# Smaller first loads, idle transposes ahead of the first product, and transposes and one projection placed earlier in a two-layer hybrid attention block

## The reference

```python
h = rms_norm(x, g_mix)                    # 256 x 1024
parts = split(h @ w_in)                   # w_in: 1024 x 10656
# branch A: sliding window attention, 8 heads, 2 key heads, rotary, per-head sinks
# branch B: low-rank q (384) and kv (256), up-projected by b_w_uq and b_w_ukv, 8 heads
# branch C: three dilated groups of 8 heads, combined by their softmax denominators
# branch M: 4 heads over rms_norm(mem) @ m_w_kv, mem of 256 x 1024, the same in both layers
y = stack([o_a, o_b, o_c, o_m]) @ w_branch                    # 4 x (512 x 1024)
x = x + (sum over branches of sigmoid(gate_pre + b_gate) * y) @ w_out
u = rms_norm(x, g_mlp) @ w_up                                 # 1024 x 4096
x = x + square(relu(u)) @ w_down                              # 4096 x 1024
```

## Time and profile before

| | us |
|---|---|
| median of 3 runs (1258.76 to 1259.2) | 1259.02 |
| profiled execution | 1258.06 |
| its span, first to last instruction | 1256.3 |
| PE busy in the span | 1231.5 (98%) |
| PE weight load busy | 1018.6 (81%) |
| DVE busy | 784.9 (62%) |
| ACT busy | 702.1 (56%) |
| POOL busy | 150.0 (12%) |
| DMA moved | 202.6 MB, mean 161 GB/s |

### The profile page before, as it was taken

How to read it: one execution, slowest core, us unless ns; L and a number is a source line. 1 busy time by engine, 2 the same in 40 slices (tenths; PEclk the granted TensorE clock), 3 DMA queues, 4 the chain that set the end, 5 groups by cost and what they waited for, 6 DMA issues and landing times.

```text
span 1256.3 us, 17554 instructions
## 1 busy us (share of the span) xinstructions
PE 1231.5 (98%) x6256; PEld 1018.6 (81%) x6256; DVE 784.9 (62%) x1222; ACT 702.1 (56%) x1086; POOL 150.0 (12%) x127
## 2 busy tenths in 40 slices
PE   7999999999999999999999999999999999999997
PEld 5788888887788878888788888888877887888886
DVE  6756768876556754444567656888655666444543
ACT  6666766654454455555566677665545454555542
POOL 6301333300000000000021113332000000000000
PEclk9999999999999999999999999999999999999999
DMA  8554545454447546656554544445544455556652
GB/s 230 188 151 123 167 129 157 151 167 145 128 130 219 178 147 185 194 184 185 177 152 154 170 140 148 121 154 168 163 141 124 147 177 182 153 185 188 191 184 71
DMA packets 110932, 202.60 MB, mean 161 GB/s; under 512 B 9984, under 2 KB 18176, under 8 KB 110848
## 3 DMA queue, kind: packets, MB, share of 16 engines
q1 hardware_dynamic: 106880, 194.12, 50.6%
q10 hardware_dynamic: 3424, 7.34, 1.7%
q0 software_dynamic: 544, 0.03, 0.1%
HBM read 200.41 MB, written 1.05 MB: 160 GB/s over the span
## 4 chain that ended last, share of the span: by engine, by line
PE 95%; DVE 2%; ACT 1%; DMA 0%; issue 0%; POOL 0%; SPq 0%; ACTq 0%; DVEq 0%
PE ps_d L1333 23%; PE ps_d L1335 22%; PE ps_d L1334 22%; PE ps_b L1333 5%; PE ps_b L1334 5%; PE ps_b L1335 5%; PE ps_b L1413 5%; PE ps_b L1367 4%; PE ps_b L1386 4%; PE ps_b L1392 2%; DMA early<-in_inv_freq_dram 0%; ACT w_hi L916 0%; DVE w_lo L1078 0%; POOL root L870 0%; ACT h_hi L992 0%
## 5 line engine op out<-in xcount | busy, mean ns | idle before, releaser
L1078 DVE TENSOR_TENSOR w_lo<-raw,w_hi 128x1024 fp32r<-128x1024 f32 (+3 forms) x380 | 450.9, 1191 | 327.1 <-ACT w_hi L916 326.1
L916 ACT ACTIVATE w_hi<-raw 128x1024 fp32r<-128x1024 f32 (+3 forms) x380 | 390.9, 1029 | 457.1 <-PE ps_d L1335 345.6
L1333 PE MATMUL ps_d<-w_hi,h_hi 128*128 128x512 f32 (+3 forms) x704 | 287.3, 408 | 3.7 <-DVE w_lo L1078 3.7
L1335 PE MATMUL ps_d<-w_hi,h_lo 128*128 128x512 f32 (+3 forms) x704 | 268.7, 382 | 0.0
L1334 PE MATMUL ps_d<-w_lo,h_hi 128*128 128x512 f32 (+3 forms) x704 | 267.6, 380 | 0.0
L1333 PE MATMUL ps_d<-w_hi,r_hi 128*128 128x512 f32 (+1 forms) x552 | 220.3, 399 | 3.7 <-DVE r_lo L1216 3.5
L1335 PE MATMUL ps_d<-w_hi,r_lo 128*128 128x512 f32 (+1 forms) x552 | 214.6, 389 | 0.0
L1334 PE MATMUL ps_d<-w_lo,r_hi 128*128 128x512 f32 (+1 forms) x552 | 214.3, 388 | 0.0
L1333 PEld LDWEIGHTS ps_d<-w_hi,h_hi 128*128 128x128 f32 x704 | 133.1, 189 | 31.0 <-issue 10.0
L1335 PEld LDWEIGHTS ps_d<-w_hi,h_lo 128*128 128x128 f32 x704 | 132.7, 188 | 25.7
L1334 PEld LDWEIGHTS ps_d<-w_lo,h_hi 128*128 128x128 f32 x704 | 133.5, 190 | 18.7
(11 more groups left out here) (154 smaller groups left out, 1262.6 us busy)
## 6 DMA issues: line engine op xcount, KB each, us to landing
raw<-in_w_in_dram SPq DMA_DIRECT2D x152, 512.0 KB, 3.6
raw<-in_w_up_dram SPq DMA_DIRECT2D x64, 512.0 KB, 3.6
raw<-in_w_down_dram SPq DMA_DIRECT2D x64, 512.0 KB, 3.7
raw<-in_w_branch_dram SPq DMA_DIRECT2D x32, 512.0 KB, 3.7
raw<-in_m_w_kv_dram SPq DMA_DIRECT2D x16, 512.0 KB, 4.4
raw<-in_w_out_dram SPq DMA_DIRECT2D x16, 512.0 KB, 3.8
early<-in_b_gate_dram ACTq DMA_DIRECT2D x16, 256.0 KB, 3.3
raw<-in_w_in_dram SPq DMA_DIRECT2D x8, 384.0 KB, 3.2
```

The lines of the kernel that those rows point to most:

```text
L916: nc.scalar.activation(w_hi[:, u % RING, 0:kn, 0:cn], raw[:, u % RAW, 0:kn, 0:cn], ACT.Copy).then_inc(hi_split, 1)
L1078: nc.vector.tensor_tensor(w_lo[:, u % RING, 0:kn, 0:cn], raw[:, u % RAW, 0:kn, 0:cn], w_hi[:, u % RING, 0:kn, 0:cn].bitcast(F32), ALU.subt ...
L1333: nc.tensor.matmul(o, hi[:, a["c"], cut], wh, start=a["first"], stop=False)
L1335: last = nc.tensor.matmul(o, lo[:, a["c"], cut], wh, start=False, stop=a["last"])
```

## The change

It does seven things. (1) The first unit is split in two of one chunk each (`fine`), and x comes in three loads: 256 and 256 columns by ACT with the gain row between, and 512 columns by SP behind the third weight load; positions and frequencies come behind the fourth. (2) PE makes 24 transposes of the identity matrix ahead of its list and 16 more ahead of the first product; nothing reads them. ACT loads the sine table at once with an activation on a zero column. (3) Two of the four x turns stand behind the first products. (4) `vC1` is projected right behind `vC0`, in both layers. (5) The turns of x for the MLP get order numbers 8 and 2 below the axis, and the row norms 4 above. (6) The last MLP group's turns get an order 8 below the axis. (7) All evictions of turns get an order 3 below, the memory turns are spread, and the plan's costs of a load and of the sines fall.

```diff
-    free = {"PE": 0.0, "ACT": 0.0, "DVE": 0.0, "POOL": 14.5, "DMA": 4.0}
+    free = {"PE": 0.0, "ACT": 0.0, "DVE": 0.0, "POOL": 14.5, "DMA": 2.4}
-        load = item("load", "DMA", kn * cn * 512 / 190e3,
+        load = item("load", "DMA", kn * cn * 512 / 300e3,
...
-        for k in range(0, kc, UC):
+        for k in [0] + list(range(1, UC)) * fine + list(range(UC, kc, UC)):
-                kn = min(UC, kc - k)
+                kn = 1 if fine and k < UC else min(UC, kc - k)
...
-        e = item("evict", "ACT", cost, [t] + lay, order=order, chain="", lay=lay, of=t, dest=dest, mode=mode, gain=gain, c=c, m=m, width=width, l=l)
+        soon = (axis[0] if order is None else order) - 3.0
+        e = item("evict", "ACT", cost, [t] + lay, order=soon, chain="", lay=lay, of=t, dest=dest, mode=mode, gain=gain, c=c, m=m, width=width, l=l)
...
-    angles = item("angles", "DVE", 2.6, [], order=-5.0, since=5.5, shift=0)
-    angles = item("angles", "DVE", 2.3, [angles], order=6.0, since=11.0, shift=1)
-    sines = item("sines", "ACT", 3.0, [angles], order=6.0)
+    angles = item("angles", "DVE", 2.6, [], order=9.0, since=9.0, shift=0)
+    angles = item("angles", "DVE", 2.3, [angles], order=12.0, since=11.0, shift=1)
+    sines = item("sines", "ACT", 0.6, [angles], order=12.0)
...
         if l == 0:
-            x_turns(0, DC, "h", "g_mix", [], ())
+            x_turns(0, half, "h", "g_mix", [], ())
+            x_turns(half, DC, "h", "g_mix", [], (), order=5.0)
...
-        aq = w_in(COL["aq"], BW, part=(0, half))
+        aq = w_in(COL["aq"], BW, part=(0, half), fine=l == 0)
...
         copy_values(v0, "vC0", "mix", True)
+        j = w_in(COL["c"] + 5 * BW, BW)
+        copy_values(j, "vC1", "mix", True)
...
-            turn(("mem", None), plain, c, 2, P, "m", "split", "m_g_mem", l)
+            turn(("mem", None), plain, c, 2, P, "m", "split", "m_g_mem", l, order=axis[0] - 8.0 + 1.4 * c)
...
         m_from = axis[0]
-        j = w_in(COL["c"] + 5 * BW, BW)
-        copy_values(j, "vC1", "mix", True)
...
-            x_turns(cg * half, (cg + 1) * half, "h", "g_mlp", list(came), tuple(half_jobs))
+            x_turns(cg * half, (cg + 1) * half, "h", "g_mlp", list(came), tuple(half_jobs), order=axis[0] - (2.0 if cg else 8.0))
+        axis[0] += 4.0
...
-            turns(tok, NW // P, P, "r%d" % (f % 2), "split")
+            turns(tok, NW // P, P, "r%d" % (f % 2), "split", order=axis[0] - 8.0 if f == UPS - 1 else None)
...
+                if u == 2:
+                    sp.dma_start(xs[:, :, NW:D], x_rows[:, :, NW:D]).then_inc(x_landed[2], 16)
+                if u == 3:
+                    sp.dma_start(pos_in.bitcast(I32), positions.rearrange("b (t p) -> p (b t)", p=P),
...
+            act.dma_start(xs[:, :, 0:2 * P], x_rows[:, :, 0:2 * P]).then_inc(x_landed[0], 16)
+            act.dma_start(g_all[:, 0, 0:DC], g_mix[0].rearrange("(c p) -> p c", p=P),
+                          allow_slow_non_contiguous=True).then_inc(g_mix_landed, 16)
+            act.dma_start(xs[:, :, 2 * P:NW], x_rows[:, :, 2 * P:NW]).then_inc(x_landed[1], 16)
+            act.wait_ge(seeded, 1)
+            nc.scalar.activation(nothing[:], no_mask[:], ACT.Sin)
...
+            def idle_turns(n):
+                for _ in range(n):
+                    nc.tensor.transpose(ps_d[:, 1, 0, 0:P], ident[:], ident[:])
             pe.wait_ge(ident_ready, 1)
+            idle_turns(24)
             for it in placed["PE"]:
                 a = it.a
+                if it is placed["PE"][2]:
+                    idle_turns(16)
```

More of the change, by code:

```diff
@@ L217, in again, with pieces @@
                 job.last = other
-    def pieces(w, rows, col, cn, l, stat, row0=0, chunk0=0, part=None, job=None):
+    def pieces(w, rows, col, cn, l, stat, row0=0, chunk0=0, part=None, job=None, fine=False):
         kc = rows // P
         job = new_job(w, cn) if job is None else job
-        for k in range(0, kc, UC):
+        for k in [0] + list(range(1, UC)) * fine + list(range(UC, kc, UC)):
             if part is None or part[0] <= k < part[1]:
-                kn = min(UC, kc - k)
+                kn = 1 if fine and k < UC else min(UC, kc - k)
                 unit(w, row0 + k * P, kn, col, cn, l, stat, chunk0 + k, k == 0, k + kn == kc, job=job)
@@ L302, in turn @@
         lay = left_homes.get(dest, []) if c == 0 else []
-        e = item("evict", "ACT", cost, [t] + lay, order=order, chain="", lay=lay, of=t, dest=dest, mode=mode, gain=gain, c=c, m=m, width=width, l=l)
+        soon = (axis[0] if order is None else order) - 3.0
+        e = item("evict", "ACT", cost, [t] + lay, order=soon, chain="", lay=lay, of=t, dest=dest, mode=mode, gain=gain, c=c, m=m, width=width, l=l)
         out = e
         if mode == "split":
-            out = item("evict_lo", "DVE", m * dve_cost(S) if gain not in (None, "half") else dve_cost(m * S), [e], order=order,
+            out = item("evict_lo", "DVE", m * dve_cost(S) if gain not in (None, "half") else dve_cost(m * S), [e], order=soon,
                        chain="", of=t, hi=e, dest=dest, gain=gain, c=c, m=m, l=l)
@@ L317, in plan, with turns @@
     left_homes = {}
-    def turns(tok, count_, width, dest, mode="plain", gain=None, l=0):
+    def turns(tok, count_, width, dest, mode="plain", gain=None, l=0, order=None):
         plain_turns[dest] = []
@@ L322, in turns @@
             done, job = tok_ready_of[tok]
-            turn(("tok", tok), [done], c, min(2, count_ - c), width, dest, mode, gain, l, home=homes[tok],
+            turn(("tok", tok), [done], c, min(2, count_ - c), width, dest, mode, gain, l, order=order, home=homes[tok],
                  ready=tok_ready_at.get(tok), scaled=scaled_at.get(tok))
@@ L471, in plan, with w_in @@
         plain = [(held["mem%d" % tt], 4.0) for tt in range(TT)]
-        def w_in(col, cn, part=None, job=None):
-            return pieces("w_in", D, col, cn, l, "h", part=part, job=job)
-        half = DC // 2
-        aq = w_in(COL["aq"], BW, part=(0, half))
+        def w_in(col, cn, part=None, job=None, fine=False):
+            return pieces("w_in", D, col, cn, l, "h", part=part, job=job, fine=fine)
+        aq = w_in(COL["aq"], BW, part=(0, half), fine=l == 0)
         v0 = w_in(COL["c"] + 2 * BW, BW, part=(0, half))
@@ L768, in hybrid_block @@
         gains_landed = sem("gains_landed")
-        x_landed, freq_landed = [sem("x_landed%d" % i) for i in range(2)], sem("freq_landed")
+        x_landed, freq_landed = [sem("x_landed%d" % i) for i in range(3)], sem("freq_landed")
+        seeded = sem("seeded")
         pool_const, dve_const, ident_ready = sem("pool_const"), sem("dve_const"), sem("ident_ready")
@@ L942, in _ @@
                         if src == "x":
-                            for c in range(2):
+                            for c in range(3):
                                 act.wait_ge(x_landed[c], 16)
@@ L976, in _ @@
                         gained = True
+                    if a["gain"] == "g_mix" and not mixed_in:
+                        act.wait_ge(g_mix_landed, 16)
+                        mixed_in = True
                     src = ps_b[0:wd, b, 0:m * S].rearrange("p (c s) -> p c s", s=S)
```

29 lines of the change are left out of this document (13 added, 16 removed).

## The result

The changed kernel took 1239.97 us (median of four runs, 1239.82 to 1241.7), against 1258.96 (four runs, 1258.76 to 1259.2): ratio 0.9852, 95% interval 0.9835 to 0.9869. The profiled execution took 1239.82 us with a span of 1238.0, against 1258.06 and 1256.3: 18.3 us less span. The profiled execution is the shortest of the four.

A forecast was written before the change was run, and what follows sets the result against it. TensorE's waits, with slow products behind those over 2 us, bound the kernel. Gains of 9.3, 5.45, 1.64 and 2.4 less 1.0 made 17.8 us: 1258.06 to 1240.3, plus 0.96, 1241.2; range 1236.5 to 1247, the forecast's own 1238.5 to 1243.5.

The forecast's parts named there:

- a first product after 11: Sign at the program's start that the prediction is wrong; the first product was expected near 9.2 us.
- new waits: In the start, behind the first product, TensorE waits of 0.7, 0.1, 1.2 and 0.6, sum 2.6 us.
- What bounds the kernel: Whole kernel: TensorE's waits, each costing idle time, 0.17 us of tail, and 1.5 to 1.6 where over 2 us.
- The MLP's x turns: Start of each MLP: turns placed earlier remove the waits for h_lo and x and the slow stretches, 9.3 us.
- The last group: Last MLP group: turns placed earlier remove the waits for r_lo and one slow stretch, 5.45 us.
- The second values: Mixer, both layers: C's second values projected between aq and its turn remove the waits there, 1.64 us.
- The `b_w_uq` turns: Mixer, both layers: the moved projection no longer covers these turns, costing 0.5 us a layer, 1.0 us.
- The start: Program start: first product at 9.15 instead of 13.02, at full pace, less 2.6 us of waits: 2.4 us gained.
- The median: Whole kernel: the median of the runs lies 0.96 us above the profiled execution, giving 1241.2 from 1240.3.
- The clock rival: Start: idle transposes don't raise the clock, so ten products are slow again; 1243.9 us, chance 0.17.
- Uncovered chains: Rival: 2 us a layer at the b_w_uq turns and 5.2 of waits in the start; 1246.8 us, chance 0.12.
- The slower side: Rival: first b_w_uq job to turn over 21.6 us spends the gain, for example 1262 at 23; chance 0.03.

The follow-up runs named there:

- c3: The changed kernel with the last group's turns back behind the last w_down unit of the group before: 1246.15 us, ratio 0.9911.
- b3: The changed kernel with the MLP's x turns and row norms at their old order numbers: 1246.52 us, ratio 0.9916.
- b4: The changed kernel with the gain row's load moved from ACT to the head of POOL's list: 1241.04 us, ratio 0.9872.
- b1: The kernel before with only the MLP's x turns (row norms behind them) and the last group's turns moved: 1250.29 us, ratio 0.9943.
- c1: The kernel before with the MLP's x turns, the last group's turns, earlier evictions and spread memory turns: 1243.13 us, ratio 0.9887.
- a4: The changed kernel with all evictions at exactly their turns' order instead of 3 below: 1241.22 us, ratio 0.9865.
- b2: The changed kernel with the projection of C's second values back behind mq: 1242.03 us, ratio 0.9880.
- a1: The changed kernel with ACT's second load of x issued ahead of the gain row instead of behind it: 1245.02 us, ratio 0.9893.
- d1: The changed kernel with c2's edit and 24 idle transposes ahead of the second x turn instead of 16 behind it: 1238.38 us, ratio 0.9848.
- a2: The changed kernel without any idle transposes, neither the 24 nor the 16: 1240.81 us, ratio 0.9858.
- a3: The changed kernel with the first 24 idle transposes but without the 16 ahead of the first product: 1239.97 us, ratio 0.9858.
- c2: The changed kernel with C's heads planned 3 later (gates_from + 11 for + 8): 1240.36 us, ratio 0.9861.

## Why the prediction was right, and where it was not

1241.2 us was forecast, 1239.97 measured, inside the narrow range. Yet one of the forecast's own signs of being wrong appeared, a first product after 11, and none of the new waits that it named came: its step on the start failed, and the total came out in part by luck. By its steps:

- **What bounds the kernel**: TensorE's waits, and the slow stretch behind those over 2 us. The first held. The second held from 40 us on: behind 1.32 us of waiting (the earlier trace rows and c3) and 1.56 (b3) the pace stayed, behind 2.19, 2.21 and 5.11 it fell. It is no fixed rule: in b4 the pace stayed behind 2.24 us at 24.73, and in the changed kernel behind 3.42 at 9.98.
- **The MLP's x turns, 9.3 us**: measured 9.1 between the traces (4.5 and 4.6), as the waits and slow stretches of the earlier trace rows are all gone. The step put all of it down to the turns' places, and b1 bears that out; the evictions' order would have saved 4.4 of it without them (b3). The forecast priced part (7) of the change at nothing. b1 and c1 show what it is worth beside the moved turns: without it 6.9 us are lost at a place that the forecast never looked at. By a4 that is not the evictions' earlier order.
- **The last group, 5.45 us**: 5.6 between the traces, 5.55 by c3.
- **The second values, 1.64 us**: both waits at aq's turn went; b2, without the move, has one of them back and two others in place of the second. **The `b_w_uq` turns, 1.0 us lost**: this step failed in its place. The first of them comes 11.65 us behind its job (120.1 to 131.75; forecast 12.2), and the chain (its last piece on VectorE ends at 130.59) fits. What the moved job uncovered stands 130 us later, the `k_c` waits, 1.4 us in both layers; b2 ties them to the move. The net is 0.3 us by these waits, 0.6 by the places of the same products in the two traces (both mixers, past the start) and 0.65 by b2. That it is near the 0.64 of the sum is luck.
- **The start, 2.4 us**: 1.9, the difference of the places of the last aq and vC0 product, with the owed memory turns. Both halves were wrong and made up for each other. The first product came at 12.14 instead of 9.15: the mis-sized step is the second load of x, forecast at 6.9 from its bytes, measured 9.94; a1 shows it at 6.56 without the gain row ahead of it. And the four new waits, 2.6 us, did not come. A first product 1.4 us earlier shows 0.47 of them (d1), and one at 10.31 shows 3.4, with pieces of weights that were put off (b4); what would come behind one at 9.15 no run shows. The 12.14 is moreover the earliest of six profiled executions with this start, in which it came as late as 13.94.
- **Not in the sum**: from TensorE's last end to the end of the span it is 3.2 us after and 4.3 before. All profiled executions with the new start have 3.2, and b1 and c1, with the old one, 4.3. It is the last store of the output: issued 0.76 us behind TensorE's last end in every one of them, it lands 2.0 us later with the new start and 3.1 with the old. No run here says why.
- **The median**: the forecast added 0.96 us to the profiled execution, the gap of the kernel before; here the gap is 0.15. That is 0.8 of the 1.2 us by which it missed.
- **The clock rival** (idle transposes don't raise the pace; it is the first in the list, and the forecast's "second rival below" is a slip) is refuted by the rows of the start and by a2. With it falls, for this kernel, the rule of the Trainium skill (TensorE: Matmul & The Clock Gate, Part 4: PE-mode transpose) that transposes do not bring the full clock; the trace disagrees, with 0.11 us a transpose at the end of the 24 where they began with 0.21.
- **Uncovered chains** cost 1.4 us in all, against 3 in the rival. **The slower side** needed a chain of over 21.6 us; it has 10.5.

The sum by the traces: 9.1 (MLP) + 5.6 (last group) + 0.6 (the mixers past the start) + 1.9 (start) + 1.1 (end) = 18.3, as measured.

## What to carry to other kernels

A late transpose costs its wait and, where the wait is long, slow products behind it: 1.5 to 1.6 us behind most waits of 2.2 us here, nothing behind those up to 1.56. Moving it up is cheap, but in a planned order look at what the plan then places one phase and one layer later. If the turns can't be moved, look at what stands between their evictions (b3). Filling idle time of TensorE with transposes nobody reads kept the pace up in both kernels that did it (d1, b4); where they stood behind it, the pace fell ahead of them or among them in five profiled executions of six. In a start, price a load by what stands ahead of it on its queue, above all loads of single elements, not by its bytes.

## What the runs showed of the hardware

Plain transposes of float32 raise TensorE's pace from 0.21 to 0.11 us each, the ratio of its two levels of 1.2 and 2.4 GHz, but when they do varies. (In the start the level is told by the pace alone: the granted clock reads 1.00 there in every window, also at 13 to 17 in the kernel before, where products take 0.43 us. At 1065 to 1068, where they take 0.43 as well, it reads 0.51.) First start of a transpose at the higher pace, the first at the lower after the idle time (none: it stayed), and the first product, in the ten profiled executions with idle transposes ahead; in all but b4 the first transpose started at 1.65 (b4: 3.31), and in a1 the idle time, 6.81 us, stands behind the second lot:

| | rose at | idle until | fell at | first product |
|---|---|---|---|---|
| after | 5.09 | 9.98 | none | 12.14 |
| a1 | 5.33 | 15.81 | 15.81 | 15.81 |
| a3 (24 only) | 4.69 | 10.29 | 11.48 | 10.70 |
| a4 | 6.59 | 10.09 | 10.09 | 13.83 |
| b2 | 6.19 | 10.12 | 10.12 | 13.68 |
| b3 | 6.19 | 9.45 | 9.75 | 13.27 |
| c2 | 7.24 | 10.17 | 10.67 | 13.94 |
| c3 | none | 10.11 | 10.93 | 13.51 |
| b4 | 6.73 | no wait | none | 10.31 |
| d1 | 7.67 | no wait | none | 10.70 |

The rise came 3.0 to 6.0 us after the first transpose, and in c3 not within 27 of them but in the idle time or just behind it. After the idle time, 2.29 to 6.81 us long, the pace fell at once or up to 1.2 us late, and in the changed kernel, with 3.42 us of it, not at all. The first product of the same start therefore came anywhere from 12.1 to 13.9, which is as wide as the spread between executions of these kernels (for example 1238.76 to 1241.01 for c2), and every comparison of them above has to be read with that in mind. With no idle time ahead of the first product (b4, d1) it did not fall.

With the load of one gain row ahead of it on the same queue, 4 KB in single elements, a 256 KB load landed 3.4 us later (9.94 against 6.56 in a1 and 6.25 in b4), and the gain row behind two such loads landed 12.2 us after its issue, against 5.3 in the second place.
